# Dense values projected in token order by pairs of weight tiles, no values stage, and the last stores awaited by GpSimd in the next stage

## The chip, the cores and the metric

One core of a Trainium2 chip. The metric is the device time of one launch in microseconds; the runs are repeated and their median is given. One more run is taken under the hardware profiler, and the rows below come from it.

## The reference

One transformer layer over 2048 tokens of width 1024. What matters here is the input projection and the first of the two token mixers:

```python
h = rmsnorm(x, norm1_g[l]) * (1.0 + sc1) + sh1
proj = jnp.einsum('bsd,de->bse', h, w_in[l])
aq, ak, av, bq, bk, bv, iq, ik, iw = split_columns(proj)
...
attn = softmax(s1) - lam * softmax(s2)          # group A, 4 heads, values av (128 wide)
o = jnp.einsum('bhqk,bkhv->bqhv', attn, v)
...
score = einsum('bqh,bqhk->bqk', w_idx, relu(q_idx . k_idx))   # group B, indexer
top_val, top_idx = lax.top_k(score, kk)         # 256 keys a query, shared key/value head bk, bv
```

The columns of `w_in` are: dense queries 0 to 511, dense keys 512 to 1023, dense values (`av`) 1024 to 1535, sparse queries 1536 to 2047, sparse keys (`bk`) 2048 to 2111, sparse values (`bv`) 2112 to 2175, and the indexer's from 2176 on. The output of the two groups goes through an output projection, a squared-ReLU MLP and a final norm.

## The kernel before

The kernel is four blocks of instructions one after the other. Every engine has its own instruction stream, and they meet at semaphores and at the boundary between blocks, which no engine passes before all have arrived.

**Index projection** (`index_projection`): norms the tokens, turns them to columns, keeps them in two parts for the split multiplication (`ht_hi`, `ht_lo`: 4 groups of 512 tokens, 8 slices of the width) and projects the indexer's columns.

**Indexing** (`indexing`, L722 to L1037): scores every admissible key for blocks 2 to 15 of 128 queries (L871), sums the 16 heads (ScalarE relu L903, VectorE L974) and looks for the 256th largest score of a query in 24 halvings. Beside it runs the rest projection: 17 tiles of 128 columns of `w_in`, called `REST_TILES`, each in four units of 512 tokens, each unit 8 parts of 3 products (L889). The weights are stationary and the tokens move, so a result is 128 columns by 512 tokens. Two slots hold the split weights of two tiles: GpSimd loads the raw tile (L811) when the rest of the tile before has been formed, ScalarE rounds it (`split`, L919), VectorE forms the rest (`lo`, L1030). A split waits until the products of two tiles before are done. ScalarE takes a unit out of PSUM (L925 and L929), VectorE forms its low part (L1034), GpSimd stores both (L820, L826). The four tiles of dense values have no low part and go to the scratch tensor `av`, columns by tokens.

The order of the instructions on each engine is written out by `indexing_plan`: it takes from the streams of `indexing_streams` the job that can begin first by its own table of costs, and among those that begin within 0.3 us the one with the lowest key. The rest projection has keys of 100 and more, so it fills where no score is ready. The loads of raw weights are not in that table. At the end of the block GpSimd waits for the last stores of all kinds (L842 to L846), and only then passes the boundary:

```python
for n in range(2):
    pool.wait_ge(s_st[n], 16 * stored[n])
    pool.wait_ge(s_mst[n], 16 * ((SPLIT - 2) // 2))
for n in range(3):
    pool.wait_ge(s_kept[n], 16 * kept[n])
```

**Values** (`values`, L1041 to L1101): SyncE loads `av` and the two parts of `bv` for 512 tokens at a time (L1067, L1069), TensorE turns each 128 tokens to rows by four transposes and two products with an identity (L1096, L1098), ScalarE and VectorE take them out to `va` and `vb` (L1076, L1082). TensorE starts on scores when all 16 tiles have been taken out.

**Attention** (`attention`, from L2453) is in the same block as the values stage. SyncE loads the queries of one unit (two dense or four sparse heads of one block, four DMAs, L2531) and the keys (L2540): first the 512 first tokens of all 8 dense key rows and of the sparse ones, 18 DMAs, then with each later unit one piece of the other tokens. The first score waits for all 18. A score (L2628) goes to `sps`, VectorE adds the bias and finds the maximum (L2841), ScalarE takes the exponential, TensorE turns the weights and multiplies them with `va` or `vb`. GpSimd stores the mixture (L2593) and loads the ranks for the search in blocks 12 to 15 (L2577). This order too is written out, by `attention_plan`. Output projection and MLP follow.

## Time and profile before

| | us |
|---|---|
| median of 3 runs | 3640.97 (3639.91 to 3645.53) |
| profiled run | 3646.88 |
| its span, first to last instruction | 3645.1 |
| TensorE busy | 3252.4 (89%) |
| VectorE busy | 2523.6 (69%) |
| ScalarE busy | 1846.2 (51%) |
| GpSimd busy | 367.9 (10%) |

The span is what the profiler saw on the core; the profiled run's own time is 1.8 us longer. PE is TensorE's matrix products and PEld its weight loads, which lie beside the products; DVE is VectorE, ACT ScalarE, POOL GpSimd and SPq the DMA issues of SyncE. A granted clock of 1.0 is 2.4 GHz, 0.5 is 1.2 GHz. Indexing lies between about 317 and 1092 us, values and the start of attention between 1095 and 1135.

### The profile page before, as it was taken

The numbers are of one execution on the slowest core, as the hardware profiler recorded it, in microseconds if no ns is written. First come the engines' busy times: TensorE is split into PE (matmuls) and PEld (weight loads), VectorE is DVE, ScalarE is ACT, GpSimd is POOL, SyncE is SP. The second block draws the span as 40 slices with busy tenths as digits, with TensorE's granted clock in tenths as the row PEclk, the third lists the DMA queues.
The fourth block names the chain that finished last, engine by engine and source line by source line (L and its number), as shares of the span: only waits on it lengthen the run. The fifth ranks groups of instructions, "written<-read, shape, count | busy, mean of one in ns | idle before, by whom it ended". The sixth has DMA issues, their size and how long they took to land. (4 is left out here: it accounts for less than half of the span.)

```text
span 3645.1 us, 44990 instructions
## 1 busy us (share of the span) xinstructions
PE 3252.4 (89%) x15808; PEld 2616.9 (72%) x15808; DVE 2523.6 (69%) x4780; ACT 1846.2 (51%) x3071; POOL 367.9 (10%) x585
## 2 busy tenths in 40 slices
PE   5996888898897798977789989799989998999999
PEld 4785666686675676755577768678868887888787
DVE  6453787878873678677676667787787775665676
ACT  4312777777664787878866743332232222322233
POOL 0010111101110000000000000011212120000141
PEclk9997998899995999989899999899999999999999
DMA  6464332222336422111111225644454445664565
GB/s 227 159 220 109 100 104 90 94 77 79 101 107 191 122 87 61 46 48 38 31 35 30 77 88 168 214 147 151 154 172 151 153 154 196 231 231 158 200 217 205
DMA packets 336409, 475.95 MB, mean 131 GB/s; under 512 B 29056, under 2 KB 220752, under 8 KB 335776
## 3 DMA queue, kind: packets, MB, share of 16 engines
q1 hardware_dynamic: 288016, 309.34, 27.0%
q0 software_dynamic: 48176, 163.83, 12.7%
q8 instruction: 123, 2.02, 0.2%
q14 instruction: 94, 0.77, 0.1%
HBM read 316.07 MB, written 156.98 MB: 130 GB/s over the span
## 5 line engine op out<-in xcount | busy, mean ns | idle before, releaser
L2145 PE MATMUL m_ps<-m_h,w_hi 128*128 128x512 f32 x1792 | 561.0, 395 | 43.3 <-DVE m_h L1774 21.0
L2145 PEld LDWEIGHTS m_ps<-m_h,w_hi 128*128 128x128 f32 x1792 | 340.8, 191 | 118.1 <-DVE m_h L1774 30.0
L974 DVE SCALAR_TENSOR_TENSOR rank<-spare,iw,rank 128x1024 f32<-128x1024 f32 (+5 forms) x330 | 332.3, 1022 | 71.6 <-ACT spare L903 65.8
L2162 PE MATMUL m_ps<-w_hi,a_hi 128*128 128x512 f32 x896 | 350.6, 391 | 12.3 <-DVE w_lo L1982 9.2
L2145 PE MATMUL m_ps<-m_h,w_lo 128*128 128x512 f32 x896 | 352.8, 394 | 0.0
L2162 PE MATMUL m_ps<-w_lo,a_hi 128*128 128x512 f32 x896 | 350.2, 391 | 0.0
L2162 PE MATMUL m_ps<-w_hi,a_lo 128*128 128x512 f32 x896 | 349.9, 390 | 0.0
L903 ACT ACTIVATE spare<-isps 128x1024 f32<-128x1024 f32 (+5 forms) x352 | 280.5, 812 | 120.5 <-PE isps L871 83.6
L871 PE MATMUL isps<-ki,iq_hi 128*128 128x512 f32 (+3 forms) x608 | 242.1, 399 | 89.3 <-ACT spare L903 67.2
L2705 ACT ACTIVATE pt<-tps 128x512 f32<-128x512 f32 (+1 forms) x432 | 233.2, 572 | 111.5 <-PE tps L2644 55.3
L2644 PE MATMUL tps<-ident,probs 128*128 128x128 f32 x1632 | 239.6, 288 | 43.4 <-DVE probs L2860 26.9
L2644 PEld LDWEIGHTS tps<-ident,probs 128*128 128x128 f32 x1632 | 191.2, 147 | 95.2 <-DVE probs L2860 34.8
L2841 DVE CUSTOM_DVE_ANT_0 probs<-sps,bias 128x1024 f32<-128x1024 f32 (+7 forms) x176 | 165.8, 962 | 126.7 <-PE tps L2644 72.6
L1562 ACT ACTIVATE a_hi<-a_lo 128x2048 fp32r<-128x2048 f32 x56 | 107.3, 1916 | 283.7 <-DMA a_lo<-dram_aop 283.7
L2693 ACT ACTIVATE probs<-probs,stat 128x128 f32<-128x128 f32 (+15 forms) x192 | 231.0, 1204 | 34.0 <-DVE stat L2850 33.7
L910 ACT ACTIVATE below<-rank,tk 128x640 int8<-128x640 f32 (+9 forms) x210 | 228.6, 1090 | 38.8 <-DVE tk L1003 35.6
L871 PE MATMUL isps<-ki,iq_lo 128*128 128x512 f32 (+3 forms) x608 | 231.2, 388 | 0.0
L889 PE MATMUL r_ps<-ht_hi,r_w_hi 128*128 128x512 f32 x544 | 221.4, 407 | 7.1 <-DVE r_ev_lo L1034 4.1
L1979 DVE TENSOR_TENSOR a_lo<-a_lo,a_hi 128x2048 fp32r<-128x2048 f32 x56 | 142.4, 2544 | 121.8 <-ACT a_hi L1562 121.7
L871 PEld LDWEIGHTS isps<-ki,iq_hi 128*128 128x128 f32 x608 | 122.5, 201 | 140.6 <-ACT spare L903 52.2
L889 PE MATMUL r_ps<-ht_lo,r_w_hi 128*128 128x512 f32 x544 | 218.6, 402 | 0.0
L889 PE MATMUL r_ps<-ht_hi,r_w_lo 128*128 128x512 f32 x544 | 217.3, 400 | 0.0
(289 smaller groups left out, 7029.4 us busy)
## 6 DMA issues: line engine op xcount, KB each, us to landing
w_raw<-in_w_ff SPq DMA_DIRECT2D x136, 512.0 KB, 5.4
dram_aop<-a_out POOLq DMA_DIRECT2D x224, 256.0 KB, 2.6
a_lo<-dram_aop SPq DMA_DIRECT2D x56, 1024.0 KB, 5.7
ada_w<-in_w_ada POOLq DMA_DIRECT2D x16, 1024.0 KB, 6.9
q_hi<-dram_proj_hi SPq DMA_DIRECT2D x128, 128.0 KB, 3.0
q_lo<-dram_proj_lo SPq DMA_DIRECT2D x128, 128.0 KB, 3.1
iq_hi<-dram_proj_hi SPq DMA_DIRECT2D x224, 64.0 KB, 2.4
iq_lo<-dram_proj_lo SPq DMA_DIRECT2D x224, 64.0 KB, 2.5
```

Of the source, the lines that this page charges most:

```text
L871: mm = nc.tensor.matmul(sps[:, job.n % 2, a:b], q[:, job.unit % IQU, job.head % 2, :], ki[:, job.c * SCH + a:job.c * SCH + b], start=part ...
L889: mm = nc.tensor.matmul(ps[:, job.n % 4, :], a[:, i % 2, job.part, :], b[:, job.g, job.part, :], start=job.part == 0 and m == 0, stop=job. ...
L903: nc.scalar.activation(spare[:, job.n % 2, 0:job.width], sps[:, job.n % 2, 0:job.width], ACT.Relu).then_inc(s_relu, 1)
L910: nc.scalar.activation(below[:, q, 0:length].bitcast(I8), ranks[job.k % 3][:, 0:length], ACT.Sign, bias=tk[:, q, TK_NT:TK_NT + 1], accum_o ...
L974: nc.vector.scalar_tensor_tensor(out=dst, in0=got, scalar=w, in1=dst, op0=ALU.mult, op1=ALU.add).then_inc(s_acc, 1)
L1979: nc.vector.tensor_tensor(s_lo[:, c % RING], s_lo[:, c % RING].bitcast(F32), s_hi[:, c % RING].bitcast(F32), ALU.subtract).then_inc(c_sl, 1)
L2145: mm = nc.tensor.matmul(ps[:, b], w[:, m % WOPS, k, :], hop[:, j, h, :, k, :], start=fresh and k == 0 and i == 0, stop=k == KH - 1 and i == 2,
L2162: mm = nc.tensor.matmul(ps[:, t], a[:, c % RING, k, t * P:(t + 1) * P], w[:, c % RING, k, :], start=first and i == 0, stop=last and i == 2 ...
L2644: tr = nc.tensor.transpose(tps[:, job.turn % TR, (2 * kk + hh) * P:(2 * kk + hh + 1) * P], probs[:, g.heads[hh] % 4, (job.first + kk) * P: ...
L2693: nc.scalar.activation(row, row, ACT.Exp, bias=stat[:, job.hm % 8, 2:3], scale=slope, accum_out=stat[:, job.hm % 8, 3:4]).then_inc(s_exp, 1)
L2705: nc.scalar.activation(pt[:, job.slot % PT, 0:width], tps[:, job.of.turn % TR, 0:width], ACT.Copy).then_inc(s_te, 1)
L2841: nc.vector.tensor_tensor_reduce(out=row[:, job.c * SCH:job.c * SCH + job.width], in0=sps[:, job.score.n % 2, 0:job.width], in1=add, scale ...
```

## The change

Three things are changed.

The dense value tiles are projected in pairs and in token order: the tokens are stationary and two tiles of weights move, 256 columns, so a unit is 256 tokens by 256 columns, 48 products instead of 24, and its result is already in rows of tokens. `av` becomes tokens by columns. The order of the rest tiles becomes 0 to 3, 8 to 11 (the values), 4 to 7, 12 to 16; a pair waits for the weights of both its tiles, and the splits of the tiles after it wait until the whole pair is done.

The values stage is deleted. GpSimd loads `va` straight from `av`, 512 tokens at a time. The sparse values are turned in the attention stage, by 8 products ahead of the first sparse score of block 0 and 24 ahead of that of block 1, in a slot of `sps`, with their operands in parts of the key buffer that are not yet in use; VectorE copies them out.

GpSimd's wait for the last stores moves from the end of the indexing block to the start of the next one, behind the two iotas; it then raises `s_settled`, on which SyncE (ahead of the sparse values) and ScalarE (ahead of `stack`) wait. SyncE loads units 0 and 1 and the dense keys before that wait, and each dense key row has a semaphore of its own for its first 512 tokens.

```diff
-        self.av = t("av", [A_HEADS * 2 * DH, SEQ])
+        self.av = t("av", [SEQ, A_HEADS * 2 * DH])
...
+VALUE_TILES = list(range(R_AV // P, R_AV // P + 4))
+OTHER_TILES = [tile for tile in range(R_IQ // P) if tile not in VALUE_TILES]
+REST_TILES = OTHER_TILES[0:4] + VALUE_TILES + OTHER_TILES[4:]
+PAIRS = [n for n in range(len(REST_TILES)) if REST_TILES[n] in VALUE_TILES[0::2]]
...
+def read_through(i):
+
+    return 4 * (i + (2 if i in PAIRS else 1))
...
-        before = [units[4 * (i - 1) - 1]] if i >= 2 else []
+        before = ([units[read_through(i - 2) - 1]] if i >= 2 else []) + ([los[i - 1]] if i - 1 in los else [])
         split = put("split", Step("split", "ACT", 1.05, 100 + i - 1.5, before, tile=tile, n=i))
-        lo = put("lo", Step("lo", "DVE", 1.25, 100 + i - 1.5, [split], tile=tile, n=i))
-        for g in range(NG):
+        los[i] = put("lo", Step("lo", "DVE", 1.25, 100 + i - 1.5, [split], tile=tile, n=i))
+        if i in PAIRS:
+            continue
+        first, weights = (i - 1, [los[i - 1], los[i]]) if i - 1 in PAIRS else (i, [los[i]] if i in los else [])
+        steps = 4 * (i + 1 - first)
+        for g in range(steps):
...
-                for n in range(2):
-                    pool.wait_ge(s_st[n], 16 * stored[n])
-                    pool.wait_ge(s_mst[n], 16 * ((SPLIT - 2) // 2))
-                for n in range(3):
-                    pool.wait_ge(s_kept[n], 16 * kept[n])
+                last_stores.extend([(s_st[n], 16 * stored[n]) for n in range(2)])
+                last_stores.extend([(s_mst[n], 16 * ((SPLIT - 2) // 2)) for n in range(2)])
+                last_stores.extend([(s_kept[n], 16 * kept[n]) for n in range(3)])
...
+                        if first in PAIRS:
+                            t, g = job.part // 4, job.g * 2 * P // GT
+                            tok = slice((job.g * 2 + t) * P % GT, (job.g * 2 + t) * P % GT + P)
+                            for k in range(job.part % 4 * 2, job.part % 4 * 2 + 2):
+                                for m, (a, b) in enumerate(((ht_hi, w_hi), (ht_lo, w_hi), (ht_hi, w_lo))):
+                                    mm = nc.tensor.matmul(ps[:, job.n % 4, t * 2 * P:(t + 1) * 2 * P], a[:, g, k, tok],
+                                                          b[:, 0:2, k, :], start=k == 0 and m == 0,
+                                                          stop=k == KT - 1 and m == 2, skip_group_check=True)
...
-def values(nc, keep, scr, late, block, va, vb):
...
             load_unit(0)
-            for dst, row in places:
-                load_keys(dst, row, 0)
+            for n in range(A_HEADS):
+                load_keys(*places[n], 0, s_first[n])
+            load_unit(1)
+            for n in range(A_HEADS, 2 * A_HEADS):
+                load_keys(*places[n], 0, s_first[n])
+            sp.wait_ge(s_settled, 1)
+            load_bv(0)
+            load_unit(2)
+            load_keys(*places[-1], 0, s_first[-1])
+            load_bv(1)
             load_chosen(2)
...
+                    if g == 1 and place == 4:
+                        sp.wait_ge(s_vt, 2)
+                    load_keys(dst, row, g, s_k[g - 1])
...
+            for signal, count in last_stores:
+                pool.wait_ge(signal, count)
+            pool.sem_inc(s_settled, 1)
+
+            def load_values(g):
+                pool.dma_start(va[:, g * TG:(g + 1) * TG, :],
+                               scr.av[g * GT:(g + 1) * GT, :].rearrange("(n p) e -> p n e", p=P)).then_inc(s_va[g], 16)
+
+            load_values(0)
...
+                    if outs % 4 == 0 and outs // 4 < NG:
+                        load_values(outs // 4)
...
-            pe.wait_ge(s_va, NB)
-            pe.wait_ge(s_vb, NB)
...
+                    if job.n in turned_at:
+                        n = turned_at.index(job.n)
+                        if n == 0:
+                            pe.wait_ge(s_idv, 1)
+                        pe.wait_ge(s_bv[n], 32)
+                        for at in range(len(turned_tiles[n])):
+                            for part in range(2):
+                                mm = nc.tensor.matmul(sps[:, job.n % 2, at * DH:(at + 1) * DH],
+                                                      bv[n][part][:, at * P:(at + 1) * P], ident_r,
+                                                      start=part == 0, stop=part == 1)
+                        mm.then_inc(s_vt, 1)
+                        pe.wait_ge(s_vb, n + 1)
...
+            nc.scalar.activation(ident_r, keep.ident[0:DH, 0:DH], ACT.Copy).then_inc(s_idv, 1)
+            act.wait_ge(s_settled, 1)
```

## Rows read from the trace of the kernel before

**Rows 1.** Busy time, share and instructions, of the page's first part.
```profile
PE 3252.4 (89%) x15808; PEld 2616.9 (72%) x15808; DVE 2523.6 (69%) x4780; ACT 1846.2 (51%) x3071; POOL 367.9 (10%) x585
```

**Rows 2.** Busiest forms on TensorE, 300 to 1095 us: busy us, mean ns, idle before.
```profile
L889 PE MATMUL r_ps<-ht_hi,r_w_hi 128*128 128x512 f32 x544 | 221.4, 407 | 7.1 <-DVE r_ev_lo L1034 4.1 <-DVE r_w_lo L1030 2.5 <-ACT r_ev_hi L925 0.3
```

**Rows 3.** Waits, 318 to 1090 us: total us, times, longest us.
```profile
PE isps L871 <- ACT spare L903: 67.2, 26, 11.6
...
ACT r_w_hi L919 <- DMA r_w_raw<-in_w_in: 6.6, 1, 6.6
```

**Rows 4.** Stretches: busy us of PE, PEld, DVE, ACT, POOL; clock, DMA share, GB/s.
```profile
320.00:1090.00 770.00, 675.64 (x2844) 538.07 (x2842) 605.29 (x1189) 552.89 (x856) 85.21 (x147) 0.93 0.31 96
...
980.00:1020.00 40.00, 39.96 (x183) 32.66 (x182) 36.35 (x34) 30.66 (x34) 2.94 (x5) 1.00 0.31 100
...
1090.00:1135.00 45.00, 26.10 (x97) 19.63 (x98) 6.11 (x21) 11.77 (x21) 3.60 (x5) 0.52 0.78 219
```

**Rows 5.** Order of time, 1087 to 1104 us: start us, duration us.
```profile
1089.17 0.39 PE L889 MATMUL r_ps<-ht_hi,r_w_lo 128*128 128x512 f32 x1
...
1090.32 0.75 DVE L1034 SCALAR_TENSOR_TENSOR r_ev_lo<-r_ps,r_scale,r_ev_hi 128x512 fp32r<-128x512 f32 x1 [4.74 <-ACT r_ev_hi L929]
...
1091.89 0.54 POOL L826 DMA_DIRECT2D dram_proj_lo<-r_ev_lo  x1
1095.59 0.40 SPq L1067 DMA_DIRECT2D av_t<-dram_av  x1
...
1102.62 1.08 PE L1096 MATMUL v_psum<-ident,av_t 128*128 128x128 f32 x4 [13.06 <-DMA bv_t<-dram_proj_lo]
```

**Rows 6.** Order of time in the values stage: one pair of L1098, the next transposes.
```profile
1103.64 0.63 PE L1098 MATMUL w_psum<-ident_v,bv_t 64*128 64x64 f32 x2
...
1104.20 0.71 PEld L1096 LDWEIGHTS v_psum<-ident,av_t 128*128 128x128 f32 x4
```

**Rows 7.** Order of time, SyncE's DMA issues, 1113 to 1131 us.
```profile
1117.15 1.26 SPq L2531 DMA_DIRECT2D q_hi<-dram_proj_hi  x2
...
1119.77 0.61 SPq L2540 DMA_DIRECT2D ka<-dram_proj_hi  x1
...
1130.65 0.59 SPq L2540 DMA_DIRECT2D kb<-dram_proj_lo  x1
```

**Rows 8.** Order of time, TensorE, the first dense and the first sparse score.
```profile
1134.82 0.45 PE L2628 MATMUL sps<-ka,q_hi 128*128 128x128 f32 x1 [5.88 <-DMA kb<-dram_proj_lo]
...
1143.06 0.41 PE L2628 MATMUL sps<-kb,q_hi 128*128 128x128 f32 x1
```

**Rows 9.** Order of time, TensorE at full clock: 512, 256 and 128 columns.
```profile
443.25 0.40 PE L871 MATMUL isps<-ki,iq_lo 128*128 128x512 f32 x1
443.48 0.28 PE L871 MATMUL isps<-ki,iq_hi 128*128 128x256 f32 x1
443.60 0.28 PE L871 MATMUL isps<-ki,iq_lo 128*128 128x256 f32 x1
443.72 0.39 PE L871 MATMUL isps<-ki,iq_hi 128*128 128x512 f32 x1
...
1667.96 1.95 PE L2665 MATMUL ops<-va,pt 128*128 128x128 f32 x16
```

**Rows 10.** The raw weight tile: its load, split and rest; ns min/median/max.
```profile
L811 POOL DMA_DIRECT2D r_w_raw<-in_w_in x17: 882/904/907, 295.7 to 938.6; - x17
L919 ACT ACTIVATE r_w_hi<-r_w_raw x17: 1044/1056/1062, 315.3 to 991.7; 128x1024 fp32r<-128x1024 f32 x17
L1030 DVE TENSOR_TENSOR r_w_lo<-r_w_raw,r_w_hi x17: 1218/1219/1225, 316.5 to 993.3; 128x1024 fp32r<-128x1024 f32 x17
...
DMA to landing us min/median/max: 4.5/4.8/5.5
```

**Rows 11.** Stretches of the early attention, columns as in rows 4.
```profile
1120.00:1140.00 20.00, 12.89 (x47) 9.87 (x46) 6.33 (x31) 7.53 (x19) 0.00 (x0) 0.50 0.97 222
...
1160.00:1180.00 20.00, 15.71 (x59) 12.43 (x60) 12.71 (x59) 11.68 (x37) 2.16 (x4) 0.50 0.43 124
```

More of the change, by code:

```diff
@@ L2450, in attention_plan, with attention @@
     return plan, by_number, freed
-def attention(nc, keep, scr, late, block, va, vb, s_va, s_vb, spent):
+def attention(nc, keep, scr, late, block, va, vb, last_stores, spent):
     plan, by_number, freed = attention_plan()
@@ L2464, in attention @@
             units[job.n_unit][2] = job.n + 1
+    TG = GT // P
+    turned_at = [min(job.n for job in by_number if job.what == "sparse" and job.block == b) for b in range(2)]
+    turned_tiles = [range(0, TG), range(TG, NB)]
     with ExitStack() as ctx:
```

162 lines of the change are left out of this document (69 added, 93 removed).

## The prediction

> **What bounds the kernel now.** I read the page's busy times first: TensorE is busy 89% of the span [rows 1], so a change gains only where TensorE waits or where it works below its usual rate. Two stretches are touched. In the indexing stage (320 to 1090 us) the reader is to see that TensorE is busy 675.6 of 770 us at a granted clock of 0.93, VectorE 605 and ScalarE 553 [rows 4]; the filler there, the rest projection, is 544 triples of 512-column products [rows 2]. Near its end TensorE is full (39.96 of 40 us in 980 to 1020 [rows 4]), so filler that comes late lengthens the stage. In the middle it is not: TensorE waits 67.2 us for ScalarE's `spare` [rows 3], since the order of the work is written out and real times lag behind it. The second stretch is the change of stage. The last product of the projection starts at 1089.17, the last store is issued at 1091.89, SyncE starts the next stage at 1095.59 and TensorE at 1102.62 [rows 5]. The values stage then turns 16 tiles, 64 transposes and 32 small products, at half clock (0.52 over 1090 to 1135 [rows 4]), and the first score comes only at 1134.82, after the last of 18 key loads [rows 7, 8]. From last product to first score: 45.6 us, all of it on the path that sets the end, because nothing of the attention stage runs beside it.
>
> **Part 1: the change of stage.** The block boundary no longer contains GpSimd's wait for the last stores. GpSimd ends its second issue at 1091.89 + 0.54 = 1092.4; with about 0.5 us for the boundary (estimate: SyncE starts 3.7 us after the issue begins, and most of that is the landing, rows 5) SyncE begins at 1093.0. Its queue now holds, in this order: the four query loads of unit 0 (2.6 us, from 1117.15 to 1119.77 in rows 7), key pairs of places 0 to 3 (1.28 us each: the first and the last of 18 issues are 10.88 us apart, 0.64 each, rows 7), unit 1 (2.6), places 4 to 7 (5.1), the wait for the last stores, two value loads of the sparse group (1.2), unit 2 (2.6), the sparse keys (1.3). The dense scores need no longer all 18 key loads but their own two. First pair issued at 1093.0 + 2.6 + 1.3 = 1096.9; the last key load in rows 7 is issued at 1130.65 and TensorE starts 4.2 us later, ScalarE's short work included, so the first score is due at about 1101: 34 us earlier. It is not the whole gain, since each next place comes 1.28 us after the last and the dense heads of block 0 now wait for keys. The sparse keys are issued at 1093.0 + 2.6 + 5.1 + 2.6 + 5.1 + 1.2 + 2.6 + 1.3 = 1113.5 and landed at 1116.7; before, the first sparse score was at 1143.06 [rows 8]. Gain up to there: 26.4 us. The wait for the stores itself sits on GpSimd, which has only the two iotas, the first values and the ranks behind it, and on SyncE and ScalarE; the stores have landed at 1095.5, long before SyncE comes to its wait at 1108.4, and ScalarE's `stack` (0.5 us) is out of the way before the first score. So I price the wait at nothing; if the landing took 10 us longer it would cost about that on ScalarE's side, less the 5 us until the first keys are in.
>
> What is against it: the loads. From 1120 to 1140 the DMA engines were already 97% busy with key and query loads alone [rows 11], and now 1 MB of dense values and 0.8 MB of ranks come on GpSimd's queue in the same 15 us. At the 222 GB/s of that row 1.8 MB is 8 us if all of it stands ahead of the sparse keys, nothing if none does. I take 2 us.
>
> The turn of the sparse values does not vanish: 32 products of the same kind stay, 8 before the first sparse score of block 0 and 24 before that of block 1, now with TensorE, and then VectorE's copy, in line. The pair of L1098 lasts 0.56 us (next start of L1096 less its own) [rows 6], so 0.28 each at half clock. The first 8 (2.2 us) run between 1112.5 and 1116.7 while the sparse keys are still landing: free. The 24 cost 6.7 us, and a copy of 128x768 about 1.1 us (estimate: VectorE takes 0.75 us for 512 columns from the same memory, rows 5), with 0.4 us of signals: about 8. Block 1 is at half clock (0.50 in 1160 to 1180) and TensorE is busy 15.7 of 20 us [rows 11], so a fifth of it falls into idle time: 6.5 on the path, between 2 (the engines that it delays had slack) and 8. The three later loads of dense values (1 MB each, behind the 4th, 8th and 12th store of the mixture) come in blocks 0 to 1 and are wanted from block 4 on; I price them at nothing, since the DMA share is falling by then (0.43 in rows 11). Likewise SyncE's wait for the second turn before the fifth piece of keys: the key pieces are needed from block 4 and the queries of two further units are already in; uncovered, it would cost the 2.6 us of a unit's issues and 3 us of landing. Sum of part 1: -26.4 + 2 + 6.5 = -18, bounds -27 and -8.
>
> **Part 2: the value tiles in token order.** Sixteen units of 24 products with 512 columns become sixteen of 48 with 256, so 384 products become 768, with a weight load each. In rows 9 a 256-column product of the same data type, each with weights of its own, is followed by the next after 0.12 us (443.48, 443.60, 443.72), and a 512-column one after 0.23 (443.25 to 443.48). 768 x 0.12 = 92.2 against 384 x 0.229 = 87.9: +4.3 us of TensorE, between 0 (two halves stream like one whole) and +8 (the next bound in rows: 0.125 by rounding of those starts). Filler that costs more lengthens the end of the stage, so all of it counts. The evacuation stays 128x512, 16 times, and the stores carry the same 256 KB in rows of half the length; a unit lasts 5.5 us or more and its buffer is awaited two units later, so that is free.
>
> The Trainium skill (TensorE: Matmul & The Clock Gate, LDWEIGHTS) gives a weight load the number of its columns divided by 1.2 in ns, which is 107 ns for 128. By that rule 384 added loads would be an estimated 41 us where nothing covers them, and this change slower. What the trace shows of it: 16 products of 128 columns, each with its own weights, take 1.95 us, 0.12 us each [rows 9], though the columns are half as many; so a load may well set the pace there, and 256 columns at 0.12 us just cover it.
>
> **Part 3: the order of the tiles.** A pair needs the weights of two tiles, and both slots hold them until its 8 units are through. Before, tile i+1 was split a whole tile ahead; now the filler has nothing to offer (a) between tile 3 and the first pair for one split and one rest, 1.06 + 1.22 us [rows 10]; (b) between the two pairs for split, rest, the load of the next raw tile (issued only after that rest: 0.9 + 4.8 [rows 10]), split, rest: 10.3 us; (c) after the second pair 2.3 us. That is 15 us without filler, in which the scores go on. Filler has about half of TensorE (544 x 3 x 0.229 = 374 of 770 us, rows 2 and 4), so 7 us of work is pushed to the end at most; since the real run lags the written order and such a gap lets it catch up, I take 2. In (b), and again behind the split of the first tile after the pairs, ScalarE stands at a split whose raw tile is still landing. That stall exists once in the trace: 6.63 us before the second split (the 6.6 us of rows 3). Two more are 13.3 us on ScalarE, with the relus, and so scores and sums, queued behind. ScalarE is idle 28% of the stage (553 of 770) and the order puts a split into such a gap; most of the landing passes there. I take 2 of 13. Sum of part 3: +4, bounds -8 and +20; the lower end is below nothing because a new written order can as well remove some of the 67 us that TensorE waits for ScalarE.
>
> **Sum.** -18 + 4 + 4 = -10 us. Against the profiled execution (3645.1 span, 3646.9 in all) that is 3636.9. The median of the runs shown, 3641.0, lies 5.9 lower, so the forecast in its terms is 3631. The later stages hold the same instructions and only start earlier.
>
> **The rivals.**
> 1. *The index stage gives it all back.* Both stalls of 6.6 us are not absorbed (+13), the 15 us without filler push 7 us to the end and the products cost 4: +24, against a part 1 of -16: +8, or 3649. It decides as soon as parts 2 and 3 are above 18. For it: TensorE is full at the end of the stage, and the written order does not know of the load's landing. Against: 28% idle on ScalarE, and 67 us of waits that a delay can hide in. In its milder form, parts 2 and 3 at +12 to +18 against -16, nothing measurable is left: 3639.
> 2. *The early keys decide less than the queue.* The attention start is bound by SyncE's issues and by 97% busy DMA, all loads land 8 us later, and block 1 pays the full 8 for its turn: part 1 is -26.4 + 8 + 8 = -10; with +8 for the rest, 3639. For it: rows 11. Against: much of what loads the DMA engines before 1120 (4 MB of values through SyncE's queue) is gone.
> 3. *Part 1 in full, order neutral.* The turn hides in block 1 (2 us), no contention, parts 2 and 3 together +2: -22, 3619. For it: only the 256-column row is a certain cost.
> 4. *The weight loads are not hidden.* The trace has 256-column products with their own weights only two in a row; in a run of 48 the loads may fall behind. By the 16 in a row, a load that nothing covers is 0.12: 384 x 0.12 = 46, -18 + 46 + 4 = +32: 3673, slower. That those 16 keep the pace of a 256-column product [rows 9] speaks against it.
>
> That the change does not do what it says would show as a values stage still there in the trace; the diff deletes it, so it gets no share.
>
> **How the numbers follow.** The forecast's own band, 3624 to 3636, gets 0.34; rival 1 0.17 for its slower form and 0.10 for the milder one; rival 2 0.15; rival 3 0.21; rival 4 0.03. Range for 8 in 10: 3611 to 3651, which takes in rivals 1 to 3. What a measurement of this kernel can tell is 0.2%, 7.3 us: faster means below 3633.7, slower above 3648.3. Faster: three quarters of the forecast's band (0.26), rival 3 and a share of rival 2 (0.24 together), with a little more from the lower end: 0.54. Slower: about 0.17. Same: 0.29.
>
> **What would show it.** Right: the first score follows the last rest product by 10 to 14 us instead of 45.6; the first sparse score 26 us or so; 24 small products and one 128x768 copy in block 1 at half clock; 768 products of 256 columns, 0.12 us apart; ScalarE waiting twice more for `r_w_raw`; the last rest product between 1085 and 1110, most likely near 1097. Wrong: 256-column starts of 0.2 us or more; a last rest product outside 1080 to 1115; the first sparse score more than 33 us behind the last rest product; or an attention stage whose length from first sparse score to last changes by more than 10 us.

## The result, and the profile after

The changed kernel takes 3669.73 us (median, 3669.20 to 3671.07), the kernel before 3643.25 us beside it on the same chip (3639.91 to 3647.95). The ratio is 1.0075, 95% interval 1.0060 to 1.0089: slower by some 27 us, where the forecast was 3631, 10 us faster than its own base. One execution of e10, among the runs further down, took 16051.62 us; without it that run's median is 3694.63 instead of 3695.12.

The profiled execution of after has a span of 3668.1 us (before 3645.1: +23.0) at a granted clock of 0.939 over the whole span (before 0.941). Landmarks of both traces, in us from the start of the span, with the differences that the rest of this text explains:

| | before | after | after - before |
|---|---|---|---|
| last index score | 1069.9 | 1067.6 | -2.3 |
| last product of the rest projection | 1089.2 | 1119.8 | +30.6 |
| first dense score | 1134.8 | 1130.1 | -4.7 |
| first sparse score | 1143.1 | 1154.1 | +11.0 |
| last sparse score | 2104.3 | 2127.4 | +23.1 |
| span | 3645.1 | 3668.1 | +23.0 |

The index stage loses 30.6, the change of stage wins 19.6 of it back (30.6 - 11.0), the early attention loses 12.1 again, and everything behind keeps the shift.

**The index stage.** Stretches of after; the columns are the busy us of PE, PEld, DVE, ACT and POOL with instructions, the granted clock, the DMA share and GB/s, as in [rows 4].

```profile
320.00:1090.00 770.00, 651.93 (x3095) 533.62 (x3094) 600.06 (x1184) 549.14 (x850) 82.80 (x137) 0.91 0.30 92
980.00:1020.00 40.00, 39.94 (x181) 32.16 (x181) 36.76 (x34) 30.63 (x34) 2.71 (x5) 1.00 0.33 102
1090.00:1125.00 35.00, 30.17 (x132) 24.41 (x130) 4.50 (x6) 4.39 (x7) 8.41 (x15) 1.00 0.30 106
1120.00:1155.00 35.00, 9.61 (x35) 7.77 (x34) 9.20 (x43) 7.35 (x24) 5.00 (x7) 0.58 0.94 223
1160.00:1180.00 20.00, 15.87 (x48) 10.32 (x48) 9.28 (x43) 9.42 (x33) 3.18 (x6) 0.50 0.68 182
```

TensorE was busy 675.64 us of the 770 in [rows 4] and is busy 651.93 now, 23.7 us less, at a clock of 0.91 instead of 0.93. That work is not gone: it comes behind 1090, where TensorE runs at full clock with almost nothing on VectorE (4.50 us) and ScalarE (4.39 us), so the rest projection alone ends the stage. Up to the last product of the stage, before and then after:

```profile
320.00:1089.60 769.60, 675.64 (x2844) 538.07 (x2842) 605.29 (x1189) 552.49 (x856) 85.21 (x147) 0.93 0.31 96
```

```profile
320.00:1120.20 800.20, 682.10 (x3226) 558.03 (x3224) 603.81 (x1189) 552.59 (x855) 88.27 (x147) 0.92 0.30 92
```

So of the 30.6 us 24.1 are time in which TensorE is not busy (118.1 against 94.0) and 6.5 are more busy time. One place where it stood in between is in the order of time around the second pair of value tiles. Start us, duration us, engine, line, and in brackets what the engine waited for:

```profile
580.60 0.28 PE L907 MATMUL r_ps<-r_w_lo,ht_hi 128*128 128x256 f32 x1
...
582.90 1.06 ACT L943 ACTIVATE r_w_hi<-r_w_raw 128x1024 fp32r<-128x1024 f32 x1
...
584.04 0.28 PE L884 MATMUL isps<-ki,iq_lo 128*128 128x128 f32 x1
...
592.30 1.22 DVE L1054 TENSOR_TENSOR r_w_lo<-r_w_raw,r_w_hi 128x1024 fp32r<-128x1024 f32 x1
593.87 0.80 PE L884 MATMUL isps<-ki,iq_hi 128*128 128x512 f32 x1 [9.56 <-ACT spare L927]
...
593.94 0.92 POOL L824 DMA_DIRECT2D r_w_raw<-in_w_in  x1
...
598.95 1.06 ACT L943 ACTIVATE r_w_hi<-r_w_raw 128x1024 fp32r<-128x1024 f32 x1 [3.84 <-DMA r_w_raw<-in_w_in]
...
600.04 1.23 DVE L1054 TENSOR_TENSOR r_w_lo<-r_w_raw,r_w_hi 128x1024 fp32r<-128x1024 f32 x1 [4.32 <-ACT r_w_hi L943]
...
601.32 0.58 PE L907 MATMUL r_ps<-r_w_hi,ht_hi 128*128 128x256 f32 x1 [5.05 <-DVE r_w_lo L1054]
```

The last filler of the first pair starts at 580.60, the first of the second at 601.32. Between them stand a split at 582.90 whose rest follows only 9.4 us later (VectorE makes the mask of a block of queries first), the load of the next raw tile, a wait of 3.84 us for its landing, a split and a rest. The scores can't fill the gap, because they wait 9.56 us for a `spare` of ScalarE. From 583 to 601 TensorE is busy for 3.7 us of 18 and the granted clock is 0.58 over the stretch:

```profile
560.00:580.00 20.00, 20.00 (x165) 19.65 (x164) 12.24 (x51) 18.90 (x36) 1.45 (x2) 1.00 0.13 41
583.00:601.00 18.00, 3.71 (x12) 2.83 (x12) 13.04 (x22) 6.79 (x12) 3.64 (x5) 0.58 0.36 109
601.00:611.00 10.00, 9.68 (x52) 8.98 (x53) 5.35 (x12) 6.87 (x14) 0.90 (x1) 0.73 0.19 52
```

The two other gaps are 508.2 to 519.6 (before the first pair) and 670.8 to 691.2 (behind the second, with scores running: TensorE is busy 14.45 us of it): 11.4 + 20.7 + 20.5 = 53 us without filler, where the forecast had 15.

These three are not the whole bill, since before has such gaps too, one of 17.9 us in the same place (583.4 to 601.3) around the same mask:

```profile
583.00:601.00 18.00, 7.21 (x26) 5.64 (x25) 17.33 (x35) 9.60 (x17) 2.53 (x4) 0.70 0.20 55
```

Counted are the stretches of over 9 us in which no filler starts: about 101 us in seven of them in before, 163 us in ten in after. Most of the difference stands behind the pairs. In before the units of the values are stored from 716.6 to 846.7, and from 653 to 833 there is no such gap, although VectorE makes two masks there (their scans, L1023, start at 710.40 and 769.68). After has tiles with a low part in that place, and gaps of 23.0 us (770.2 to 793.1) and 25.5 us (842.6 to 868.1) around its masks (scans, L1047, at 775.49 and 852.53). A unit with a low part needs VectorE, a unit of values does not, so values can run past a mask; that this is the reason was not tried by itself.

Over the whole stage the waits of after are (total us, times, longest us):

```profile
PE isps L884 <- ACT spare L927: 82.0, 40, 11.3
...
ACT r_w_hi L943 <- DMA r_w_raw<-in_w_in: 10.6, 2, 6.8
...
PE r_ps L907 <- DVE r_w_lo L1054: 8.6, 2, 5.1
```

TensorE waits 82.0 us for `spare`, 67.2 before [rows 3]: 14.8 more. ScalarE at raw tiles: 10.6 against 6.6, one wait and 4 us more.

**The change of stage.** Order of time in after, the last product of the index stage being the one that starts at 1119.8:

```profile
1122.51 0.54 POOL L841 DMA_DIRECT2D dram_proj_lo<-r_ev_lo  x1
1122.88 1.26 SPq L2504 DMA_DIRECT2D q_hi<-dram_proj_hi  x2
...
1125.54 0.61 SPq L2513 DMA_DIRECT2D ka<-dram_proj_hi  x1
...
1126.94 0.78 POOL L2563 DMA_DIRECT2D va<-dram_av  x1 [1.76 <-issue]
...
1128.91 0.54 POOL L2575 DMA_DIRECT2D rank_in<-dram_ranks  x1 [1.19 <-issue]
...
1130.08 0.44 PE L2643 MATMUL sps<-ka,q_hi 128*128 128x128 f32 x1 [9.91 <-DMA ka<-dram_proj_lo]
...
1135.75 0.48 PE L2643 MATMUL sps<-ka,q_hi 128*128 128x128 f32 x1 [5.02 <-DMA ka<-dram_proj_lo]
...
1154.10 0.47 PE L2643 MATMUL sps<-kb,q_hi 128*128 128x128 f32 x1 [0.52 <-DVE vb L2850]
```

The reader is to see that SyncE begins 0.37 us after the last store is issued (3.70 before, [rows 5]), that the first dense score follows the last product by 10.3 us (45.6 before), and that TensorE then stands at one pair of keys after the other: over 1120 to 1290 it waits 22.9 us for `ka`, in 7 places, the 9.9 us of the first included. The DMA engines are 94% busy from 1120 to 1155 (223 GB/s), and the first sparse score comes 34.3 us after the last rest product (53.9 before).

**Behind the first sparse score.** Block 1 in after:

```profile
1178.02 0.52 ACT L2748 ACTIVATE mixst<-tps,rinv 128x64 f32<-128x64 f32 x2 [3.20 <-DMA dram_mix<-mixst]
...
1185.64 5.33 PE L2627 MATMUL sps<-ka 64*128 64x64 f32 x24
...
1191.00 0.96 DVE L2850 COPY vb<-sps 128x768 f32<-128x768 f32 x1 [5.09 <-PE sps L2627]
...
1210.14 0.52 ACT L2748 ACTIVATE mixst<-tps,rinv 128x64 f32<-128x64 f32 x2 [5.37 <-DMA dram_mix<-mixst]
```

The second turn costs 5.33 us on TensorE and 0.96 on VectorE, with VectorE waiting. Twice ScalarE waits longer for a store of the mixture to land, 3.20 and 5.37 us; the longest such wait of before is 1.7 us. These small stores share GpSimd's queue with loads of 1 MB of dense values; e5 tries whether that is the reason.

### The profile page after: what moved, and what is told of

It is laid out like the page before. It is cut to its first block and busy times, and to the rows that moved or that the text cites. A ratio compares the mean times of both kernels' runs of the same rounds, so it can differ in the third digit from the quotient of the medians.

```text
span 3668.1 us, 45591 instructions
## 1 busy us (share of the span) xinstructions
PE 3240.1 (88%) x16128; PEld 2623.7 (72%) x16128; DVE 2520.5 (69%) x4766; ACT 1838.1 (50%) x3055; POOL 376.2 (10%) x589
## 5 line engine op out<-in xcount | busy, mean ns | idle before, releaser
L934 ACT ACTIVATE below<-rank,tk 128x640 int8<-128x640 f32 (+9 forms) x210 | 228.7, 1090 | 21.4 <-DVE tk L1027 16.1
L1499 ACT ACTIVATE w_hi<-w_raw 128x512 fp32r<-128x512 f32 x128 | 79.9, 624 | 249.7 <-DVE w_raw L1768 241.3
L2123 PEld LDWEIGHTS m_ps<-w_hi,a_hi 128*128 128x128 f32 x896 | 169.3, 189 | 48.8 <-issue 9.3
L1410 POOL DMA_DIRECT2D dram_aop<-a_out x224 | 121.4, 542 | 769.8 <-DVE a_out L1872 387.7
```

Of the source, the lines that this page charges most:

```text
L934: nc.scalar.activation(below[:, q, 0:length].bitcast(I8), ranks[job.k % 3][:, 0:length], ACT.Sign, bias=tk[:, q, TK_NT:TK_NT + 1], accum_o ...
L1410: pool.dma_start(scr.aop[op, row:row + P, half * GT:(half + 1) * GT], act_in[:, op, :]).then_inc(q_a[op], 16)
L2123: mm = nc.tensor.matmul(ps[:, t], a[:, c % RING, k, t * P:(t + 1) * P], w[:, c % RING, k, :], start=first and i == 0, stop=last and i == 2 ...
```

## The experiments

What stood open after the result, in theories of which the runs had to choose. For the 30.6 us of the index stage: *the written order* (the pairs make gaps without filler, and what is not placed there is pushed behind the last score); *the products* (256 columns with weights of their own cost more than 0.12 us); *the stalls* (ScalarE at raw tiles holds the scores up). For the change of stage: *the loads* (values and ranks beside the keys) and *the stores* (queued behind value loads). In the table "us" is the median of the timed runs and the ratio is against before on the same chip. "Parts" is what the written order itself holds of the rest projection behind its last score, in parts of three products, six for those of a pair (the expectations name the numbers); the other columns are from each one's trace: start of the last index score, of the last rest product, from the later of the two to the first sparse score, and from there to the last sparse score.

| kernel | parts | last score | last rest | to sparse | attention | us | ratio, 95% |
|---|---|---|---|---|---|---|---|
| before | 28 | 1069.9 | 1089.2 | 53.9 | 961.2 | 3643.25 | 1 |
| after | 76 | 1067.6 | 1119.8 | 34.3 | 973.3 | 3669.73 | 1.0075, 1.0060 to 1.0089 |
| e1_stage_only | 28 | 1064.0 | 1083.3 | 33.0 | 971.6 | 3639.13 | 0.9988, 0.9978 to 0.9998 |
| e2_order_no_pairs | 48 | 1075.2 | 1108.1 | 33.8 | 972.9 | 3655.80 | 1.0028, 1.0017 to 1.0039 |
| e3_pairs_wide | 76 | 1066.3 | 1118.4 | 35.7 | 975.1 | 3668.72 | 1.0070, 1.0053 to 1.0087 |
| e4_splits_first | 5 | 1094.9 | 1098.3 | 33.6 | 971.3 | 3645.82 | 1.0006, 0.9996 to 1.0015 |
| e5_values_on_sync | 76 | 1070.4 | 1122.6 | 34.2 | 969.9 | 3669.84 | 1.0071, 1.0055 to 1.0088 |
| e6_order_landing | 8 | 1083.9 | 1089.4 | 35.3 | 971.6 | 3639.71 | 0.9983, 0.9973 to 0.9993 |
| e7_order_early_pairs | 0 | 1096.9 | 1069.7 | 37.1 | 974.4 | 3649.10 | 1.0011, 1.0001 to 1.0020 |
| e8_sync_and_late_ranks | 76 | 1072.8 | 1124.9 | 32.2 | 978.4 | 3668.15 | 1.0058, 1.0041 to 1.0075 |
| e9_pairs_at_12 | 43 | 1064.4 | 1096.9 | 33.9 | 972.4 | 3648.93 | 1.0011, 1.0000 to 1.0021 |
| e10_pairs_first | 100 | 1073.8 | 1143.8 | 35.0 | 974.3 | 3695.12 | 1.0132, 1.0112 to 1.0152 |
| e11_best_order_sync | 8 | 1082.6 | 1088.1 | 36.9 | 970.0 | 3635.74 | 0.9969, 0.9954 to 0.9984 |
| e12_light_start | 8 | 1084.1 | 1089.6 | 29.7 | 977.1 | 3635.21 | 0.9974, 0.9963 to 0.9986 |

e1 to e4 ran on one chip (before 3645.0 there), e5 to e8 on another (3645.82), e9 to e12 on a third (3644.95). All edits are against after.

The table holds the mechanism. From the last score to the last rest product it is 19.2 us in before, 52.2 in after, 33.0 in e2, 3.4 in e4, 5.5 in e6, 32.5 in e9 and 70.0 in e10: nearly parts x 0.68 us each time, 0.68 being the plan's price of a part. So this tail is no accident of the run but stands in the written order.

**e1: the change of stage alone.** Order and products of before, boundary and attention of after. The dense values are stored columns by tokens here and in e2 and e3, so attention takes them from the wrong places.

```diff
-REST_TILES = OTHER_TILES[0:4] + VALUE_TILES + OTHER_TILES[4:]
-PAIRS = [n for n in range(len(REST_TILES)) if REST_TILES[n] in VALUE_TILES[0::2]]
+REST_TILES = list(range(R_IQ // P))
+PAIRS = []
 ...
-                        pool.dma_start(scr.av[tok, row:row + 2 * P].rearrange("(t p) e -> p t e", p=P),
-                                       ev_hi[:, job.n % 2, :].bitcast(F32).rearrange("p (t e) -> p t e", t=2)
-                                       ).then_inc(s_st[job.n % 2], 16)
+                        pool.dma_start(scr.av.rearrange("(a b) e -> a (b e)", b=4)[row:row + P, job.g * GT:(job.g + 1) * GT],
+                                       ev_hi[:, job.n % 2, :].bitcast(F32)).then_inc(s_st[job.n % 2], 16)
```

> The changed kernel with the projection of before: tiles in the order 0 to 16, no pairs, 512-column products; the value tiles are stored as they come, columns by tokens, so the dense values that attention reads are in the wrong places. It leaves the change of stage alone. The order theory (the 30.6 us by which the last rest product moved come from the written order of the pairs) and the product theory (they come from the 256-column products and from ScalarE waiting for raw tiles) both expect the last rest product at 1089 to 1091 us. From there the first sparse score should follow by 34 us as in the changed kernel, and attention should be 12 us longer than before: 3643 - 19.6 + 12 = 3636. If the forecast's price of the change of stage was right after all (-18) and the changed kernel's loss in attention came with the pairs, 3625.

Measured: 5.9 us less than before (3639.13 against 3645.0; by the interval of the ratio 0.7 to 8). Expected were 3636, or 3625 if the forecast's price was right. So part 1 gains, but about a third of the forecast's 18; to the first sparse score it is 33.0 us as in after, and the attention is 10.4 us longer than before's. The index stage ended 5.9 us earlier than before's although its order is the same: that much a stage varies between executions, and differences of a few us in the table's trace columns say nothing.

**e2: the order of the tiles, without pairs.** As after, with `PAIRS = []` and the store of e1.

> As the run with the change of stage alone, but with the changed kernel's order of tiles (0 to 3, values, 4 to 16), still without pairs and with 512-column products; dense values in the wrong places. The written order now has 48 parts of filler behind the last score, against 28 before and 76 in the changed kernel. Order theory: each part is 0.68 us, so the last rest product comes 20 x 0.68 = 13 us later, 1103, total 3649. Product theory: nothing differs from the run before, 3636.

**e3: pairs, with products of 512 columns.** The order, the units and the stores of after, only the products changed: 24 a unit instead of 48.

```diff
-                            t, g = job.part // 4, job.g * 2 * P // GT
 ...
+                            for m, (a, b) in enumerate(((w_hi, ht_hi), (w_hi, ht_lo), (w_lo, ht_hi))):
+                                mm = nc.tensor.matmul(ps[:, job.n % 4, :], a[:, job.g // 4, job.part, :],
+                                                      b[:, job.g % 4, job.part, :],
+                                                      start=job.part == 0 and m == 0, stop=job.part == KT - 1 and m == 2,
+                                                      skip_group_check=True)
```

> The changed kernel with its written order and all its waits for pairs, but each part of a value unit is three products of 512 columns with stationary weights as before, instead of six of 256; dense values in the wrong places. Order theory: last rest product at 1116 to 1120, total 3666 to 3670, the difference to the changed kernel being the price of the 256-column products, 0 to 4 us. Product theory: most of the 30 us goes, 3640 to 3645.

Measured, both: e2 3655.80, 16.7 above e1 and more than the 13 expected; e3 3668.72, 12.9 above e2 and as expected. After is 1.0 above e3 by medians, 2.8 when each is taken against before on its own chip; the last rest products are 1.4 apart. So the order of the tiles costs 17 without a single pair in it, the pairing 13 (each give or take some 5, by the intervals of the ratios), and the products 1 to 3. The theory of the products falls. TensorE's time without work in the stage, 94.0 us in before and in e1, is 112.8 in e2 and 116.7 in e3; its busy time is 675.8 in e2 and 682.2 in e3, where the clock over the stage is lower (0.91 against 0.93). How the products run in after:

```profile
L907 PEld LDWEIGHTS r_ps<-r_w_hi,ht_hi x256: 187/188/330, 519.6 to 670.4; 128*128 128x128 f32 x128
L907 PE MATMUL r_ps<-r_w_hi,ht_hi x256: 276/281/580, 519.6 to 670.5; 128*128 128x256 f32 x128
```

One form of three (ns min/median/max, first and last start): the median product takes 0.281 us in the records, as the 0.28 of [rows 9], and at full clock the next starts 0.12 us later.

**e4: splits as early as they can be.** The split and the rest of a tile get the first rank of the plan instead of nearly the last.

```diff
-        split = put("split", Step("split", "ACT", 1.05, 100 + i - 1.5, before, tile=tile, n=i))
-        los[i] = put("lo", Step("lo", "DVE", 1.25, 100 + i - 1.5, [split], tile=tile, n=i))
+        split = put("split", Step("split", "ACT", 1.05, -1, before, tile=tile, n=i))
+        los[i] = put("lo", Step("lo", "DVE", 1.25, -1, [split], tile=tile, n=i))
```

> The changed kernel, computing all, with the keys of the split and of the rest of a weight tile set to -1, so that they come ahead of the scores' work on ScalarE and VectorE as soon as their slot is free. The written order has 5 parts behind the last score instead of 76. Order theory: the gaps without filler shrink, the last rest product comes within 5 us of the last score, 1068 to 1090, total 3620 to 3645. Product theory: ScalarE now stands at more splits whose raw tile has not landed, last rest product at 1115 or later, 3665 or more.

Measured: 3645.82, 23.9 us better than after, though with the same pairs and products in the same tile order. The tail behind the last score shrank from 52.2 us to 3.4. The gap between the pairs is now the forecast's 10.3 us, the one behind them is below 9, and only the one before them stays (11.3 us):

```profile
573.66 0.28 PE L907 MATMUL r_ps<-r_w_lo,ht_hi 128*128 128x256 f32 x1
...
583.93 0.58 PE L907 MATMUL r_ps<-r_w_hi,ht_hi 128*128 128x256 f32 x1 [8.18 <-DVE r_w_lo L1054]
```

But the scores end 27 us later. One reason is plain: TensorE is busy 670.4 us up to its last score, 629.9 in after, since the work of the tail now stands ahead of it. A split also goes ahead of relus wherever it can, even where its raw tile is not in:

```profile
PE isps L884 <- ACT spare L927: 70.0, 24, 13.4
DVE r_w_lo L1054 <- ACT r_w_hi L943: 31.6, 13, 6.6
...
ACT r_w_hi L943 <- DMA r_w_raw<-in_w_in: 15.4, 3, 6.9
```

Waits over 318 to 1125 us. ScalarE waits 4.8 us more at raw tiles than in after (10.6), but TensorE waits less for `spare` (82.0 in after). So that the stalls are what ends the scores late is not shown.

**e6: a plan that knows of the landing.** Pairs behind 11 other tiles, splits at rank 8, and no split before its raw tile can be there.

```diff
-REST_TILES = OTHER_TILES[0:4] + VALUE_TILES + OTHER_TILES[4:]
+REST_TILES = OTHER_TILES[0:11] + VALUE_TILES + OTHER_TILES[11:]
 ...
-        split = put("split", Step("split", "ACT", 1.05, 100 + i - 1.5, before, tile=tile, n=i))
-        los[i] = put("lo", Step("lo", "DVE", 1.25, 100 + i - 1.5, [split], tile=tile, n=i))
+        split = put("split", Step("split", "ACT", 1.05, 8, before, tile=tile, n=i))
+        los[i] = put("lo", Step("lo", "DVE", 1.25, 8, [split], tile=tile, n=i))
 ...
+        elif job.kind == "split" and job.n:
+            if streams["lo"][job.n - 1].end is None:
+                return None
+            t = streams["lo"][job.n - 1].end + 7.0
```

> The changed kernel, computing all, with another written order: the values as tiles 11 to 14 of the row, key 8 for the splits and rests, and a split not planned before the landing of its raw tile (7 us after the rest before it). It has 8 parts of filler behind the last score, and no split is written ahead of a landing. Order theory: the run with splits first had few parts behind the last score too, but stood at splits for raw tiles, so its scores ended 27 us late; here both are cured, last score at 1065 to 1078, last rest product at 1070 to 1085, total 3625 to 3635. If the 27 us of that run came from splits taking ScalarE's and VectorE's time ahead of scores and not from the landing, the scores end at 1085 or later, total above 3640.

**e7: the same with the pairs early** (behind 5 tiles, rank 5).

> As the run before, with the values as tiles 5 to 8 and key 5. No part of filler is left behind the last score, and the last score stands in the written order where it stood before. Order theory: last score at 1070 to 1085 and all filler before it, total 3625 to 3635. The place of the pairs itself matters nothing by this theory; if early pairs cost (no scores ready to fill the gaps), 3650.

Measured: e6 ends its stage at 1089.4, like before, with the 256-column products in it, and takes 3639.71, 30.0 us less than after: the whole loss of the index stage is an order's. It changes place, rank and landing together, and the landing alone was not tried. ScalarE has no wait at a raw tile left, yet the last score comes at 1083.9 where 1065 to 1078 were expected, and the total is above the 3625 to 3635 of the order theory: the theory said where the loss was, not how much could be won. TensorE in 320 to 1090 us:

```profile
320.00:1090.00 770.00, 675.55 (x3226) 555.19 (x3224) 604.93 (x1189) 553.30 (x856) 87.83 (x147) 0.93 0.31 95
```

675.55 us busy at 0.93, as in [rows 4]: at an even clock the products cost TensorE nothing that this shows. e7 has no filler at all behind the last score, yet its scores end at 1096.9 where 1070 to 1085 were expected, and it takes 3649.10, the price named for the case that early pairs cost. So half of the theory fails there: no tail is not enough, since work moved ahead of the last score delays it. The scores then set the end.

**e9 and e10: the place of the pairs alone.** One line each, ranks as in after.

```diff
-REST_TILES = OTHER_TILES[0:4] + VALUE_TILES + OTHER_TILES[4:]
+REST_TILES = OTHER_TILES[0:12] + VALUE_TILES + OTHER_TILES[12:]
```

and `VALUE_TILES + OTHER_TILES` in e10.

> The changed kernel with one line changed: the values are tiles 12 to 15 of the row instead of 4 to 7. Written by the same plan, 43 parts of filler stand behind the last score instead of 76, and by the plan's own table the stage ends 30 us earlier than the changed kernel's and 2 us later than before. Order theory: last rest product at 1087 to 1095, total 3636 to 3645. If pairs cost their three gaps wherever they stand: 1110 or later, 3660 or more.

> The changed kernel with the values as the first four tiles: 100 parts behind the last score, by the plan's own table 10 us later than the changed kernel's. Order theory: last rest product at 1126 to 1134, total 3676 to 3682. If pairs cost the same wherever they stand: 1120, 3669.

Measured: the same pairs moved late cost 21 us less (3648.93, expected 3636 to 3645), moved to the front 25 us more (3695.12, expected 3676 to 3682). Both directions are as the order theory has them, both are slower than it said. TensorE's waits for `spare` over 318 to 1125 us in e10 and, below, e9:

```profile
PE isps L884 <- ACT spare L927: 120.6, 45, 11.6
```

```profile
PE isps L884 <- ACT spare L927: 69.8, 26, 8.9
```

120.6 us, 82.0 in after, 69.8 in e9 (67.2 in [rows 3]): early, when score tiles are short and ScalarE's part is the larger, TensorE has nothing else to do in a gap; late it has. That the share of ScalarE is why was not tried by itself; with the place of the pairs that of all other tiles changes too.

**e5: three value loads on SyncE's queue.** GpSimd's queue then carries the stores of the mixture alone.

```diff
+                if n in (9, 11, 13):
+                    g = (n - 7) // 2
+                    sp.dma_start(va[:, g * TG:(g + 1) * TG, :],
+                                 scr.av[g * GT:(g + 1) * GT, :].rearrange("(n p) e -> p n e", p=P)).then_inc(s_va[g], 16)
 ...
-                    if outs % 4 == 0 and outs // 4 < NG:
-                        load_values(outs // 4)
```

> The changed kernel with its three later loads of dense values (1 MB each) taken from GpSimd's queue, where the stores of the mixture stand behind them, and issued by SyncE with units 9, 11 and 13. Theory of the store behind the load: in the changed kernel ScalarE waits 3.2 and 5.4 us for a store behind such a load; both waits go, attention from the first to the last sparse score falls from 973 by 5 to 7 us, total 3663. Rival, that the loss in attention is only the turn of 24 products in block 1 and the loads cost nothing: 973 stays, 3669.

Measured: the attention is 3.4 us shorter (969.9, expected 5 to 7), the waits of ScalarE's copy of the mixture (L2748, here L2750) for its stores fall from 16.5 only to 14.0 us (10.1 in before), and the total doesn't move (3669.84, expected 3663). The wait of 3.20 us is 1.26 now, but the long one stays, with the value loads on the other queue:

```profile
1211.30 0.52 ACT L2750 ACTIVATE mixst<-tps,rinv 128x64 f32<-128x64 f32 x2 [6.45 <-DMA dram_mix<-mixst]
```

So standing behind a load in GpSimd's queue is not its reason. A value load is in flight then too (issued at 1200.57), on the same DMA engines; whether that is the reason is open.

**e8: e5, and the ranks loaded behind the first store of the mixture.**

```diff
-                if job.kind == "fetch":
-                    if job.block > SPLIT:
-                        pool.wait_ge(s_mask, job.block - SPLIT)
+                if job.kind == "fetch" and job.block > SPLIT:
+                    pool.wait_ge(s_mask, job.block - SPLIT)
 ...
+                    if outs == 1:
+                        pool.dma_start(rank[:, 0:P * (SPLIT + 1)],
+                                       scr.ranks[0, :, 0:P * (SPLIT + 1)]).then_inc(s_rank, 16)
```

> As the run with the values on SyncE's queue, and the first load of ranks (0.8 MB) is issued after the first store of the mixture instead of beside the first keys. Contention theory: TensorE's 22.9 us of waits for dense keys at the start of attention are partly ranks and values on the same DMA engines; 0.8 MB at 222 GB/s is 3.7 us, so the first sparse score follows the last rest product by 30 to 31 us instead of 34.3, total 3 us less than the run with values on SyncE. Rival, that SyncE's issues set the pace and not the engines: no change in that distance.

Measured: to the first sparse score 2.1 us less (32.2, expected 30 to 31), and 8.4 us more from there to the last (against e5); 3668.15, no gain that its interval shows. The execution in the trace took 3677.83, 9.7 above the median, so the 8.4 us are not shown to be the edit's.

**e11: e6 with e5; e12: e11 with a light start** (of the first value load only the first 128 tokens; the rest of it and the ranks behind the first store of the mixture).

```diff
-            load_values(0)
+            pool.dma_start(va[:, 0, :], scr.av[0:P, :]).then_inc(s_va[0], 16)
 ...
+                    if outs == 1:
+                        pool.dma_start(va[:, 1:TG, :],
+                                       scr.av[P:GT, :].rearrange("(n p) e -> p n e", p=P)).then_inc(s_va1, 16)
```

> The order with the landing in it (3639.7 against 3645.8 of before) and the three later value loads issued by SyncE. The run with these loads on SyncE alone shortened attention from 973.3 to 969.9 us: total 3636 to 3638. If that difference was noise: 3640.

> As the run before, and GpSimd loads only the values of the first 128 tokens (256 KB) ahead of the first scores; the other 768 KB and the ranks (832 KB) follow the first store of the mixture. Contention theory: 1.6 MB less on the DMA engines while the dense keys land, 1.6 MB at 222 GB/s is 7 us; putting off the ranks alone gave 2.1 us. First sparse score 27 to 30 us behind the last rest product instead of 34 to 35, total 3631 to 3634. Rival, that the key loads saturate the engines by themselves: distance 32 or more, total unchanged or later, because the values are then late for the second block.

Measured: 3635.74 and 3635.21, the two best of the study, 9 us under before and faster than it by interval (e11 as expected, e12 just outside its 3631 to 3634). Between the two there is no difference in the medians that counts. e12's light start brings the first sparse score 7.2 us closer to the end of the index stage (29.7 against 36.9): the loads do compete. Stretch 1100 to 1120 us of e11, then of e12:

```profile
1100.00:1120.00 20.00, 5.98 (x20) 4.60 (x20) 5.54 (x33) 4.02 (x18) 0.14 (x1) 0.50 1.09 256
```

```profile
1100.00:1120.00 20.00, 9.22 (x34) 7.58 (x34) 6.32 (x37) 4.62 (x19) 1.85 (x3) 0.50 0.85 213
```

A DMA share of 1.09 becomes 0.85, TensorE's busy time rises from 5.98 to 9.22 us, and its waits for `ka` fall from 23.2 to 14.6 us. But the attention is 7.1 us longer, and the last sparse score comes at 2096.4 against 2095.0: what is won at the start is lost again at once, by a wait for queries that e11 does not have:

```profile
1132.18 0.48 PE L2655 MATMUL sps<-kb,q_hi 128*128 128x128 f32 x1 [7.98 <-DMA q_lo<-dram_proj_lo]
```

The put-off loads (value rest and ranks, issued from 1113.63 on, 12.1 and 15.4 us to landing) are in flight just there; that they hold the queries up was not tried.

## Why the prediction was wrong, point by point

- **The step that failed: part 3, the order of the tiles.** Priced at +4 with bounds of -8 and +20; the stage lost 30.6 us, of which 1 to 3 are part 2, so part 3 is +28 or +29, beyond its own bound. Three things in the step failed. First, it has no term for the move of the value tiles itself: 16.7 us, e2 against e1, with no pairs in either. The traces suggest why (units without a low part pass the masks, and they now stand elsewhere); that was not tried by itself. Second, the gaps at the pairs, (a), (b), (c), were priced at the durations of their instructions (2.3, 10.3, 2.3), and the trace shows 11.4, 20.7 and 20.5. I priced what an operation takes, not when the plan lets it run: with the first rank for split and rest (e4) (b) is 10.3 and (c) is below 9. The pairing in all is 12.9 us, e3 against e2. (a) stays at 11.3 in e4; why is open. Third, "7 us of work is pushed to the end at most, and I take 2": the tail behind the last score grew by 33 us (52.2 against 19.2), as the 76 parts against 28 of the written order say. Nothing of it was caught up: TensorE is 24.1 us longer without work and 6.5 us longer busy, at a lower clock (0.92 against 0.93).
- **A sum that would come out by luck.** Half of the 53 us of the three gaps is 26, close to 29. It is no explanation: before has 101 us of gaps of this kind, one of 17.9 us where (b) stands, and more than half of the loss is there without pairs.
- **What could have been read ahead.** The plan is a program, and it prices both kernels by its own table: the changed stage ends 32 us later (30 + 2, in the expectation of e9), against 30.6 measured. It is not exact for every order (10 us from after to e10, where the last rest products are 24.1 apart), but I guessed part 3 where it could be run.
- **"The upper end +20"** was built from stalls of 13.3 us. They came once more and not twice, with 4 us (10.6 against 6.6), so taking little for them was right, for a term that didn't matter.
- **Part 2, 256-column products: +4.3, range 0 to 8.** Measured 1 to 3 (1.0 and 2.8 by medians, 1.4 by the last rest products), in the range; the intervals of the ratios are wider than that and do not exclude the 4.3. The Trainium skill's 107 ns for a weight load (TensorE: Matmul & The Clock Gate, LDWEIGHTS) stays hidden: e3 and after differ by 1 to 3 us with 384 loads between them, where the estimate by the page's rule was 41. Rival 4 falls.
- **Part 1, up to the first sparse score: -26.4 + 2.** Measured -19.6 against a forecast of -24.4. The start is as forecast (SyncE 0.37 us behind the last issue, first dense score 10.3 us behind the last product, forecast 10 to 14). The 2 us for the loads was mis-sized: e12, which takes most of them away, is 7.2 us shorter than e11.
- **Part 1, the second turn: +6.5.** Measured 5.33 + 0.96 us with VectorE waiting, 6.3. Right in mechanism and, as far as one trace can say it, in size; no run takes the turn out.
- **Part 1, loads of values and stores "priced at nothing".** The attention from first to last sparse score grew by 12.1 us, 5.8 more than the turn. Two waits of ScalarE for a store (3.20 and 5.37 us) stand there; e5 takes the value loads off that queue and gains 3.4 in the trace, nothing in the total, and the longer wait stays. So the queue may be some of the 5.8, and what the rest is stays open. Part 1 in all: -19.6 + 12.1 = -7.5 in the traces, -5.9 by the medians of e1, against -18 with bounds -27 and -8. This term too failed, by its upper bound.
- **The sum.** -7.5 + 30.6 = +23.1, the shift of the last sparse score and, to 0.1 us, of the span. The forecast had -18 + 8 = -10.
- **The rivals.** Rival 1 (the index stage gives it all back) named the right place and sign, with 3649 for a price: its 7 us of pushed filler was a tail longer by 33, its 13 us of stalls 4. Three of the four things named as what would show the forecast wrong came: a last rest product outside 1080 to 1115 (1119.8), a first sparse score more than 33 us behind it (34.3) and an attention changed by more than 10 us (12.1).

## What to carry to other kernels

When an order is written out ahead, the cost of a moved step is read from where the plan puts it, not from how long it takes; where the plan is a program, run it for both kernels and count what it leaves behind the last step of the other work. Filler left there comes back whole at the end, where nothing runs beside it (48 more parts, 33 us more here). Moving tiles without changing any work cost some 17 us here, making pairs of them some 13. Look at the busy time of the bound engine over the stage (here 675.6 to 651.9 us) before anything else, and hold a gap of the new trace against the same place in the old one before calling it new. A stage boundary opened for early loads gains less than the distance it removes: price each next user of the loads, and check whether the engine that is freed early is held up later.

## What was not expected of the hardware

- In the middle of the stage TensorE's granted clock went from 1.00 (560 to 580) to 0.58 over a stretch of 18 us in which it was busy for 3.7, and was still at 0.73 over the next 10 us, in which it was busy 9.68. Before has the same dip in a milder form (0.70 over 583 to 601, busy 7.21). In the 10 us of 0.73 the first 256-column products started 0.21 us apart instead of 0.12 (601.70 and 601.91 in the trace).
- One core's DMA engines can be the bound of a short stretch: shares of 0.94 to 1.09 at 223 to 256 GB/s, with the key loads that TensorE awaits taking part in it.
